# Rounded passes on every mixer chunk: halves of chunks rounded by ScalarE, remainders shared between VectorE and GpSimd

## What is computed

```python
h = rmsnorm(x, norm_mix_g[l])
z = h @ w_in[l]                       # columns for A, B, C, D and four gates of 1024
y_a, y_b, y_c, y_d = spatial_gating(z_a), pooling(z_b), rwkv7(z_c), ssd(z_d)   # 512 wide each
proj = einsum('btkc,kcd->btkd', branches, w_branch[l])
merged = sum_k sigmoid(z_g)_k * proj_k
x = x + merged @ w_out[l]
h = rmsnorm(x, norm_ffn_g[l])
x = x + (swiglu(h) if l == 0 else moe_top2_of_8(h))    # hidden width 3584
```

## Time and profile before

| | |
|---|---|
| three runs, median | 2349.38 us (2345.57 to 2350.28) |
| the profiled execution's own time | 2349.66 us |
| its span in the trace | 2347.6 us |
| TensorE busy, share of the span | 2235.1 us, 95% |
| VectorE, ScalarE, GpSimd busy | 1433.7, 1052.7, 51.6 us |
| mean granted TensorE clock | 0.96 |

### The profile page before, as it was taken

One profiled execution on the slowest core, in us unless ns is written; L12 is line 12 of the kernel. 1 busy time (PEld: TensorE's weight loads), 2 busy tenths in 40 slices (PEclk: granted clock), 3 DMA queues, 4 the chain that ended last, 5 costly groups with the idle time before them and its releaser, 6 DMA issues.

```text
span 2347.6 us, 30978 instructions
## 1 busy us (share of the span) xinstructions
PE 2235.1 (95%) x12088; PEld 1825.8 (78%) x12088; DVE 1433.7 (61%) x1395; ACT 1052.7 (45%) x886; POOL 51.6 (2%) x52
## 2 busy tenths in 40 slices
PE   7979999989999897999998899999999999999997
PEld 6868889879999786888977677777777777777775
DVE  3544643235553453554222788888888888888885
ACT  4312211123333432211111577777777767777673
POOL 0100000000000010000010000000000000000000
PEclk9979999989999998999898899999999999999999
DMA  7422212325455342321131498989999999989892
GB/s 299 173 72 108 90 55 72 141 108 180 179 179 182 123 144 72 128 76 67 54 126 72 181 368 330 365 341 356 349 347 349 349 347 348 368 329 367 330 367 108
DMA packets 69342, 504.66 MB, mean 215 GB/s; under 512 B 7696, under 2 KB 7952, under 8 KB 8208
## 3 DMA queue, kind: packets, MB, share of 16 engines
q1 hardware_dynamic: 68832, 500.57, 56.9%
q10 hardware_dynamic: 432, 2.95, 0.3%
HBM read 502.44 MB, written 1.05 MB: 214 GB/s over the span
## 4 chain that ended last, share of the span: by engine, by line
PE 93%; DVE 3%; ACT 1%; issue 1%; DMA 0%; SPq 0%; DVEq 0%; ACTq 0%
PE g L433 61%; PE m L433 30%; PE m L466 1%; PE m L903 1%; DVE h L1354 1%; DMA ring<-stream 0%; DVE arena L1572 0%; DVE rstd L1352 0%; DVE arena L1570 0%; ACT w_high L1167 0%; ACT arena L1006 0%; ACT L1009 0%; DVE h L1871 0%; DVE arena L1432 0%; DVE arena L1428 0%
## 5 line engine op out<-in xcount | busy, mean ns | idle before, releaser
L1750 DVE TENSOR_TENSOR ring_low<-ring,we_high 128x2048 fp32r<-128x2048 f32 x336 | 769.1, 2290 | 153.3 <-ACT we_high L1212 152.9
L1212 ACT ACTIVATE we_high<-ring 128x2048 fp32r<-128x2048 f32 x336 | 644.2, 1918 | 273.8 <-PE g L433 180.9
L433 PE MATMUL g<-we_high,hg_high 128*96 128x512 f32 x896 | 358.4, 400 | 10.3 <-DVE ring_low L1750 10.3
L433 PE MATMUL g<-ring_low,hg_high 128*96 128x512 f32 x896 | 353.8, 395 | 0.0
L433 PE MATMUL g<-we_high,hg_low 128*96 128x512 f32 x896 | 352.6, 394 | 0.0
L433 PE MATMUL g<-h,ring 128*128 128x256 f32 x1472 | 338.2, 387 | 0.0
L433 PEld LDWEIGHTS g<-h,ring 128*128 128x128 f32 x1472 | 282.3, 194 | 42.2 <-issue 4.3
L433 PE MATMUL m<-arena 128*128 128x128 f32 (+7 forms) x1832 | 264.7, 309 | 20.1 <-DVE arena L1428 9.4
L433 PEld LDWEIGHTS m<-arena 128*128 128x128 f32 (+3 forms) x1832 | 235.6, 195 | 47.2 <-issue 14.7
L433 PE MATMUL g<-h_high,w_high 128*128 128x256 f32 x768 | 220.3, 287 | 27.0 <-DVE h_low L1667 25.1
L433 PE MATMUL g<-h_low,w_high 128*128 128x256 f32 x768 | 219.0, 285 | 0.0
(11 more groups left out here) (240 smaller groups left out, 2224.4 us busy)
## 6 DMA issues: line engine op xcount, KB each, us to landing
ring<-stream SPq DMA_DIRECT2D x472, 1024.0 KB, 4.8
cc<-cc_in SPq DMA_DIRECT2D x1, 2352.5 KB, 16.4
sw<-sw_in SPq DMA_DIRECT2D x1, 1088.0 KB, 11.2
sw<-sw_in ACTq DMA_DIRECT2D x1, 1088.0 KB, 6.2
x<-x_in SPq DMA_DIRECT2D x1, 1024.0 KB, 4.8
out<-h ACTq DMA_DIRECT2D x1, 1024.0 KB, 3.9
rep<-rep_in SPq DMA_DIRECT2D x1, 768.0 KB, 17.8
rep<-rep_in ACTq DMA_DIRECT2D x1, 768.0 KB, 7.7
```

The costliest lines, as they stand in the source:

```text
L433: return pe.matmul(o, a, b, start=start, stop=stop, skip_group_check=True)
L1212: A(we_high[n % 3][:, :], ring[:, slot, :], ACT.Copy).then_inc(high_ready, 1)
L1750: TT(ring_low[:, slot, :], ring[:, slot, :], we_high[n % 3][:, :], ALU.subtract).then_inc(low_ready, 1)
```

## The change

All 47 chunks of a mixer go through `three`. The rounded weights no longer lie in two slots of a chunk but in `z_w`, five slots of half a chunk (N_SLOTS = 5, HALF = 1024). A half b of chunk n is number 2n + b; ACT may write it when PE has used the half five numbers earlier (`half_free`, counted by `half_used` and `chunks_used`). DVE makes the remainders of chunks 0 to 11 (N_DVE = 12), as before, now in halves, those of chunks 8 to 11 between the taps of its convolution as before. POOL makes those of chunks 12 to 46 (`lows`), in its own order with the pooling, with the additions of the merge and with the remainders of the branch outputs A, B and D. ACT rounds the branch outputs (`y_split`); DVE makes the remainder of C's, adds up the last four gated products itself and makes the remainders of `mg`.

The memory for it is found by smaller constants (`cc` ends where the pooling counts began, 1633 columns of its second load rather than 4705), by h's remainder in h's own place, and by RING = 6. In mixer C the sums over a head (ss, va) are taken into 8 rows, and are spread over the partitions by a new product (sr, vr) after the square root and reciprocal, which run on 8 rows rather than 128. SIDE gets the points "sr" and "vr", with four quarters each, and "kt" has four rather than eight. The out chunks run by halves, the first halves of chunks 0 and 1 ahead of their second. The dense layer's gate and up chunks are written out 28 times; before they were a loop of two turns of 14.

```diff
-RING = 7
+RING = 6
+N_SLOTS = 5
+HALF = 1024
+N_DVE = 12
...
-SIDE = [("cw", 12), ("ss", 4), ("bo", 12), ("kt", 8)]
+SIDE = [("cw", 12), ("ss", 4), ("bo", 12), ("sr", 4), ("kt", 4)]
...
-SIDE += [("mu", 4), ("va", 4)]
+SIDE += [("mu", 4), ("va", 4), ("vr", 4)]
...
-                sp.dma_start(cc[:, first:NCC], cc_in[:, first:NCC]).then_inc(all_consts_in, 16)
+                sp.dma_start(cc[:, first:N_KEPT], cc_in[:, first:N_KEPT]).then_inc(all_consts_in, 16)
+                sp.dma_start(early[:, :, :], counts[:, :, 0:EARLY]).then_inc(all_consts_in, 16)
...
@@ merge_quarters (PE)
-                            last = mm(gb(("gate", step, unit))[:, j * T:(j + 1) * T], w[:, DT * j + k, :], h[:, k, :],
-                                      k == 0, k == DT - 1)
+                            last = three(gb(("gate", step, unit))[:, half * T:(half + 1) * T], wh[:, quarter, k % 4, :], wl[:, quarter, k % 4, :],
+                                         h_high[:, k, :], h_low[:, k, :], k == 0, k == DT - 1)
...
@@ merge (PE)
-                for i in range(N_OUT):
+                for i, b in ((0, 0), (1, 0), (0, 1), (1, 1), (2, 0), (2, 1), (3, 0), (3, 1)):
...
@@ evacuate, gates (ACT)
+                    z_highs(l, 2 * n + 1 + N_SLOTS)
                     act.wait_ge(chunks_used, unit_chunk(l, unit) + 1)
...
+                    z_highs(l, 2 * n + 2 + N_SLOTS)
...
+                for q4 in range(lo, hi):
+                    (step, i), part = MERGE_CHUNKS[q4 // 4], q4 % 4
+                    z_highs(l, 2 * NZ + q4 // 2 + N_SLOTS)
...
+            def z_high(l, n, b):
                 c = chunk0(l) + n
                 act.wait_ge(landed[c % RING], 16 * (c // RING + 1))
+                half_free(act, l, n, b)
+                A(half_slot(l, n, b), half_ring(ring, l, n, b), ACT.Copy).then_inc(z_high_ready, 1)
...
@@ the mixer's norm (ACT)
-                     lambda ins: drain(l, "norm1", ins), lambda: (z_high(l, 0), z_high(l, 1)))
+                     lambda ins: drain(l, "norm1", ins), lambda: z_highs(l, N_SLOTS))
...
@@ POOL
+            def lows(l, lo, hi):
+                for n in range(lo, hi):
+                    for b in range(2):
+                        if (n, b) == (NZ + 1, 1):
+                            y_lows(l, 0)
...
+                        pool.wait_ge(z_high_ready, 2 * (l * N_MIX + n) + b + 1)
+                        G.tensor_tensor(half_ring(ring_low, l, n, b), half_ring(ring, l, n, b), half_slot(l, n, b), ALU.subtract)\
+                            .then_inc(pool_low_ready, 1)
...
@@ mixer_c (DVE)
-                q.step(V.reciprocal(va[:, :, :], va[:, :, :]))
-                q.step(TT(oo[:, :, :], oo[:, :, :], va[:, :, :], ALU.mult))
+                q.step(V.reciprocal(rstd[0:H, :], rstd[0:H, :]), S["vr_ready"])
+                side("mu", "vr")
```

More of the change, by code:

```diff
@@ L93 @@
 CC_LIST = [("ones", T), ("eps", 1), ("gn_eps", 1), ("ident", P), ("heads", P), ("strict_up", P), ("incl_up", P), ("low2", P), ("up2", P),
-           ("off", LEVELS * P), ("count", 4 * T), ("reset", 4 * T), ("sel", H * P), ("slots", CAP), ("slot", 1)]
+           ("off", LEVELS * P), ("slots", CAP), ("slot", 1), ("count", 4 * T), ("reset", 4 * T), ("sel", H * P)]
+WINDOWS = (2, 4, 8, 16)
+EARLY = 16
 CC, _n = {}, 0
@@ L460, in two_banks, with head_sums, over_heads @@
                     fill(l, f"{name}{i}", last)
+            def head_sums(l, stage, src):
+                m_free(pe, l, stage)
+                for j in range(4):
+                    last = mm(mb(stage)[0:H, 0:T], by_head[:, j, :], src[:, j, :], j == 0, j == 3)
+                fill(l, stage, last)
+            def over_heads(l, name):
+                two_banks(l, name, lambda j: spread[:, j * P:(j + 1) * P], lambda j: rstd[0:H, :])
             def turn(l, stage, parts):
@@ L472, in project @@
                     name, i = Z_UNITS[n]
[L473 to L496, removed]
-                            for k in range(DT):
[L498 to L503, removed]
-                                                 k == 0, k == DT - 1)
-                                else:
-                                    last = mm(o, w[:, DT * j + k, :], h[:, k, :], k == 0, k == DT - 1)
@@ L721, in merge_quarters @@
                     (step, unit), part = MERGE_CHUNKS[n // 4], n % 4
-                    w = chunk(chunk0(l) + NZ + n // 4)
+                    half, quarter = part // 2, part % 2
+                    wh, wl = halves(l, NZ + n // 4, half)
                     if unit < 2:
@@ L1148, in gates @@
+                side("vr")
             def gates(l, lo, hi):
-                for n in range(2 * STEPS):
-                    step, i = n // 2, n % 2
-                    if lo < 4 * MERGE_CHUNKS.index((step, i)) + 4 <= hi:
-                        unit = ("gate", step, i)
-                        act.wait_ge(chunks_used, unit_chunk(l, unit) + 1)
-                        if step < STEPS - 1 and 2 * STEPS * l + n > 1:
-                            act.wait_ge(merged, 2 * STEPS * l + n - 1)
-                        q.add(A(sg_of(step, i), gb(unit)[:, :], ACT.Sigmoid), g_drained[G_PLAN[unit][0]])
@@ L1169, in split_h, with y_split @@
+            highs = [0]
+            def y_split(l, branch):
+                for i in range(2):
+                    if branch == 2:
+                        act.wait_ge(S["yc_ready"], 2 * l + i + 1)
+                    two = slice(2 * i, 2 * i + 2)
+                    A(y_high[:, two, :], (yA, yB, yC, yD)[branch][:, two, :], ACT.Copy).then_inc(S["y_high_ready"], 1)
             def split_h(n):
@@ L1485, in side @@
                     products(l, SIDE_AT[first][0], SIDE_AT[last or first][1])
+                for c in range(NCH):
+                    m_done(dve, l, f"a{c}")
+                q.step(V.tensor_copy(spread.rearrange("p (h m) -> p h m", h=H), along(ident[0:H, 0:H], 64)), S["spread_ready"])
                 for i in range(CT // 2):
```

435 lines of the change are left out of this document (288 added, 147 removed), and 4 rows, old and new, of the table M_USES.

## The result

The changed kernel takes 2366.66 us (median of 4 runs, 2366.14 to 2367.31), the kernel before beside it 2347.48 (2345.11 to 2350.28): a ratio of 1.0081, interval 1.0064 to 1.0099. I predicted 2330, in 2285 to 2362, and faster. It is slower, by 19 us.

A forecast was written before the change was run, and what follows sets the result against it. TensorE was taken as the bound, busy 2235.1 of 2347.6 us. Terms -79.2 + 3.6 - 12.5 + 9.6 + 6.4 + 37 + 13 + 2.6 = -19.5 gave span 2328, launch 2330 us, range 2285 to 2362.

The forecast's parts named there:

- Items 1 and 2: Mixer chunks: 70 more in three passes, -79.2 us; new spread products, dt product and unrolled dense loop, together +3.6.
- Item 4: Start and layer 1's norm: five half chunks rounded ahead of the square root delay it, 8.2 and 1.4, together +9.6 us.
- Item 5: Mixers D and A: half-chunk roundings ahead in ScalarE's queue and a shorter covering chunk, 3.2 us a layer, +6.4.
- item 6: GpSimd's remainders block VectorE instructions with two SBUF inputs in mixer C and norms: 18.5 us a layer, +37, bounds 0 and 75.
- Item 3: Out chunks by halves: 5.8 us of cover removes TensorE's whole wait and the clock loss, -12.5 us.
- Item 7: Mixer C's output before pj6: too little cover, TensorE idles 5 us and loses 1.5 by clock a layer, +13.
- the additions: GpSimd's additions standing behind halves in its queue delay `mg`: +2.6 us in all.
- Rival B: GpSimd becomes the pacer, a half exceeding TensorE's 2.89 us, so TensorE waits for every half: 2365 us, 2343 to 2380; chance 0.25.

The follow-up runs named there:

- The edit that undoes it: Changed kernel, but ScalarE rounds four half chunks, not five, ahead of the mixer norm's square root: 2356.76 us.
- without GpSimd's reads: Changed kernel, but each of GpSimd's 140 half-chunk remainders replaced by three memsets of similar total length, reading nothing from SBUF: 2289.97 us.
- the last experiment: The kernel with the five edits, plus GpSimd remainders in 512-column pieces and mg's first parts rounded ahead of the last half chunk: 2282.94 us.
- the experiment on it alone: Changed kernel, but GpSimd does nothing during mixer C's shift and mix; VectorE makes three half-chunk remainders and branch A's: 2329.19 us.
- the kernel with the five edits: Changed kernel: four half chunks before norm's root, mix free of GpSimd, mixer C's and D's exponentials earlier, GpSimd held until v is normed: ratio 0.9873.

## Why the prediction was wrong

- **Items 1 and 2, the saved work: right.** 1.17 us saved on a side chunk. That only 54.4 us show in TensorE's busy time is the clock, which I had charged at the out chunks and before pj6 alone.
- **Item 4, the start: right.** The first product is 8.5 us later (8.2 predicted), layer 1's norm 1.1 (1.4). The edit that undoes it gives 10.
- **Item 5, mixers D and A: the sum right by luck.** TensorE's wait in D went from 3.0 to 5.5 us and that for L1103 from 1.7 to 2.6: 3.3 us a layer, 3.2 predicted. But without GpSimd's reads D's wait is 4.0 in the first layer and 4.2 in the second, so the order of ScalarE's queue costs some 2 us a layer and the lock the rest. And ahead of mixer A's first product, which this item names too, TensorE waits 6.1 us where it waited 2.9 (3.1 without the reads), and 1.9 more ahead of its second. By the lock these norm parts cost some 6 us a layer; item 6 had 2.5.
- **Item 3, the out chunks: wrong.** I took 5.8 us of cover against a chain of 4 to 5. But mg's rounding stood behind a half chunk that ScalarE may write only when TensorE has finished the last branch chunk, so the cover was over before the chain began; 4.3 us of wait stay in each layer where there were 3.8 (2.5 without GpSimd's reads), and the chunks behind lose 1.7 to the clock. I had read ScalarE's order at the two places where it delays a start, and not here. By the last experiment the order is worth 7 (traces) to 12 us (medians) once nothing else ends later; changed alone it gave 4.
- **Item 6, the lock: right mechanism, wrong size, and it decided the sign.** This is the step that failed. I priced 37 us between bounds of 0 and 75; without GpSimd's reads 77 come off, where items 6 and 7 with the additions had been put at 52.6. The largest part is the mix: I took 9 us over, because I thought VectorE would often run on once it had the pair. It alternates, one instruction each, for as long as GpSimd has work: 16.8 us over, more even than the 13.7 that I gave for alternating and for which the prediction has no working. With the colder clock behind it the mix cost some 16 us a layer, and the experiment on it alone gives 37 where I had 18. The price of a chain is the number of its instructions that can be blocked, for as many as GpSimd has ready in a row, times GpSimd's instruction. I had read GpSimd as busy for four fifths, and had named the wait for branch A that holds up its queue, but not seen that nine instructions would then follow without a gap. For the stretch from `ss` to `kt` I had 3.5 a layer; the wait at "sr" alone is 5.4 (1.1 without the reads), where exponentials moved behind branch B's rounding and two lengthened products end last. And I left tensor_scalar out of the count.
- **Where the whole miss lies.** The kernel without GpSimd's reads takes 59 us less than the kernel before; by items 1 to 5 it should take 72.1 less. So 13 of the 37 us by which I missed (2330 against 2366.7) are not the lock: the waits that stay without it are 3.5 us ahead of pj6 and 2.5 ahead of the out chunks, 12 in both layers, and at both ScalarE's queue ends last. The other 24 are the lock.
- **Item 7, before pj6: right, with a second cause beneath.** 5 us of idle predicted, 5.5 measured. Behind C's output the changed kernel's timeline has

```profile
466.00 2.51 DVE L1749 TENSOR_SCALAR arena<-arena,pp 128x256 f32<-128x256 f32 x4
...
469.81 3.36 DVE L1757 TENSOR_TENSOR arena<-arena 128x512 f32<-128x512 f32 x2
473.26 3.26 DVE L1761 TENSOR_TENSOR y_low<-arena,y_high 128x512 fp32r<-128x512 f32 x2
```

```profile
472.60 1.23 ACT L1241 ACTIVATE y_high<-arena 128x512 fp32r<-128x512 f32 x2
```

  The first instruction of each of VectorE's three lines is held up by a half of GpSimd, by 1.1, 2.1 and 2.0 us: 5.2, and some 5 was forecast. The chain of waits names GpSimd there, but its remainder ends at 475.4; VectorE's ends at 476.52, and TensorE starts at 476.62. C's rounding also stands behind a half chunk that waited for TensorE, as mg's does, but starts 0.04 us after the product that it rounds, so here the order costs nothing. Without GpSimd's reads it does: the products end at 435.4, the rounding starts 3.1 us later,

```profile
438.54 1.14 ACT L1241 ACTIVATE y_high<-arena 128x512 fp32r<-128x512 f32 x2
```

  and 3.5 us of TensorE's wait stay.
- **Rival B had the time (2365) and not the reason.** GpSimd's half took 2.47 us on average (the longest 3.35), and TensorE waited 3.1 us for it in all. What was real of B is that the mix and the convolution alternate, which makes VectorE late and not GpSimd. B's own sum was off too: 70 is the number of chunks, and a wait at every half would count 140.

By the Trainium skill ("SBUF — State Buffer", Who interferes with whom) the pair of ports is held for a whole instruction and the other engine blocks fully; the traces agree on both sides, and the rule that such waits hit GpSimd too is in the 4.1 us of its branch remainder. The same section of the Trainium skill has tensor_scalar and copies among those that can take the shared pair of read and write ports, and two SBUF inputs contending only with a GpSimd instruction that reads; the memsets that held up L1628, and not the two-input products, agree.

What stays open: how much of the 77 us is each engine's own delay, since the experiment took away both; and whether pieces smaller still would gain.

## What to carry to other kernels

Before work is moved to GpSimd, list the VectorE instructions that read SBUF twice, or that are tensor_scalar or copies, on the chains that run at the same time, and charge each with one whole GpSimd instruction, up to the number that GpSimd will have ready in a row. What helps is keeping GpSimd out of the two or three stretches that end last, and cutting its instructions short. Then read each engine's queue for what stands ahead of the last step of a chain: an early load or rounding that waits for TensorE turns cover into wait.

## What the runs showed of the hardware

- While both had work the two engines alternated one for one: 14 instructions of 0.40 us took 22.4 us beside 9 of GpSimd, in both layers.
- A tensor_scalar of one SBUF input is blocked as well: 0.55 us became 2.47, four of 0.29 took 9.76. It is also held up by GpSimd's memsets (four took 3.63 us), while two-input instructions were not: the two norm products of mixer A stayed at 0.69 us beside them, the multiply-adds at 0.47.
- A copy of 128x1024 from SBUF, 0.69 us alone, took 2.71 beside GpSimd's halves in both layers of the kernel with the five edits (mixer D, L1565).
- A tensor_tensor of 128x512 with an input from PSUM kept 0.69 us in every run.
- Idle time of TensorE costs again as clock: for the same matmuls it was busy 2180.7 us at a mean granted clock of 0.938, and 2148.9 us at 0.957 where its waits were 47 us shorter.
